# Two experts' weight units in runs of four in a two-layer encoder trunk

## The reference

```
logits = (t @ router)
top_v, top_i = lax.top_k(logits, TOP_K);  w = softmax(top_v)
for e in range(N_EXPERTS):
    out = out + combine[:, e:e + 1] * swiglu(t, w_gate[e], w_up[e], w_down[e])
swiglu(h, g, u, d) = (silu(h @ g) * (h @ u)) @ d        # g, u: 1024 x 3584, d: 3584 x 1024
```

## Time and profile before

| | us |
|---|---|
| median of 3 runs | 1401.47 |
| lowest, highest | 1400.12, 1403.07 |
| the profiled execution, device time | 1400.06 |
| its span, first to last instruction | 1398.0 |
| PE busy | 1369.0 (98%) |
| DVE busy | 737.5 (53%) |
| ACT busy | 632.1 (45%) |
| mean granted PE clock | 0.998 |

### The profile page before, as it was taken

The page is one execution under the profiler, slowest core; times in us unless marked ns, Lnnn a source line. Parts: engine busy times, 40 slices in busy tenths (PEclk is TensorE's granted clock), DMA queues, the critical chain, the costliest instruction groups (busy, mean ns, idle before and its releaser), DMA issues.

```text
span 1398.0 us, 16533 instructions
## 1 busy us (share of the span) xinstructions
PE 1369.0 (98%) x6427; PEld 928.7 (66%) x6427; DVE 737.5 (53%) x626; ACT 632.1 (45%) x574; POOL 28.9 (2%) x34
## 2 busy tenths in 40 slices
PE   7999999999999989999999999999999999999998
PEld 7978888888888865555565555565555556555555
DVE  6975544446733464554555554545545455455455
ACT  5855333444555345444444444444344445444443
POOL 2000000001200000000000000000000000000000
PEclk9999999999999999999999999999999999999999
DMA  9456555555440069999999999999999999999995
GB/s 335 166 178 229 180 181 186 196 190 163 149 141 1 15 253 409 412 415 415 399 414 398 365 413 413 407 399 393 362 404 413 406 410 397 374 387 414 414 399 245
DMA packets 127885, 434.83 MB, mean 311 GB/s; under 512 B 6960, under 2 KB 9120, under 8 KB 113472
## 3 DMA queue, kind: packets, MB, share of 16 engines
q1 hardware_dynamic: 127344, 433.11, 80.9%
q0 software_dynamic: 368, 0.63, 0.2%
q10 hardware_dynamic: 96, 0.03, 0.0%
HBM read 432.69 MB, written 1.05 MB: 310 GB/s over the span
## 4 chain that ended last, share of the span: by engine, by line
PE 82%; DMA 8%; ACT 4%; DVE 3%; issue 2%; DVEq 0%; SPq 0%; POOL 0%; ACTq 0%
PE ps L1320 18%; PE ps L1307 11%; PE ps L1308 9%; PE ps L838 9%; PE ps L1309 9%; PE ps L840 8%; PE ps L839 8%; DMA ring<-in_moe_w_gate_dram 5%; DVE wlo L1466 2%; DMA ring<-in_moe_w_down_dram 2%; ACT whi L487 2%; PE ps L1239 1%; PE ps L1230 1%; PE ps L1068 1%; DMA ring<-in_moe_w_up_dram 1%
## 5 line engine op out<-in xcount | busy, mean ns | idle before, releaser
L1466 DVE TENSOR_TENSOR wlo<-ring,whi 128x2048 fp32r<-128x2048 f32 x168 | 384.7, 2291 | 345.2 <-ACT whi L487 341.6
L487 ACT ACTIVATE whi<-ring 128x2048 fp32r<-128x2048 f32 x168 | 321.4, 1914 | 405.6 <-DMA ring<-in_moe_w_up_dram 153.4
L1320 PE MATMUL ps<-ring,xl 128*64 128x512 f32 (+1 forms) x1024 | 217.1, 550 | 2.3 <-issue 1.7
L1458 DVE TENSOR_TENSOR wlo<-raw,whi 128x2048 fp32r<-128x2048 f32 x73 | 166.5, 2288 | 73.5 <-PE ps L840 71.4
L1307 PE MATMUL ps<-whi,hT_hi 128*128 128x512 f32 x448 | 188.5, 421 | 8.4 <-DVE wlo L1466 7.7
L480 ACT ACTIVATE whi<-raw 128x2048 fp32r<-128x2048 f32 x73 | 139.4, 1916 | 84.8 <-PE ps L840 82.9
L1308 PE MATMUL ps<-wlo,hT_hi 128*128 128x512 f32 x448 | 177.1, 395 | 0.0
L1309 PE MATMUL ps<-whi,hT_lo 128*128 128x512 f32 x448 | 174.9, 390 | 0.0
L838 PE MATMUL ps<-whi,hT_hi 128*128 128x512 f32 x384 | 153.2, 399 | 2.4 <-DVE wlo L1458 1.4
L1307 PEld LDWEIGHTS ps<-whi,hT_hi 128*128 128x128 f32 x448 | 83.9, 187 | 105.8 <-issue 50.2
L840 PE MATMUL ps<-whi,hT_lo 128*128 128x512 f32 x384 | 149.7, 390 | 0.0
(11 more groups left out here) (312 smaller groups left out, 1328.0 us busy)
## 6 DMA issues: line engine op xcount, KB each, us to landing
ring<-in_moe_w_gate_dram SPq DMA_DIRECT2D x112, 1024.0 KB, 10.0
ring<-in_moe_w_up_dram SPq DMA_DIRECT2D x112, 1024.0 KB, 10.0
ring<-in_moe_w_down_dram SPq DMA_DIRECT2D x112, 1024.0 KB, 10.4
raw<-in_fox_w_in_dram SPq DMA_DIRECT2D x16, 1024.0 KB, 5.2
raw<-in_ffn_w_gate_dram SPq DMA_DIRECT2D x14, 1024.0 KB, 5.2
raw<-in_ffn_w_up_dram SPq DMA_DIRECT2D x14, 1024.0 KB, 5.1
raw<-in_ffn_w_down_dram SPq DMA_DIRECT2D x14, 1024.0 KB, 5.0
raw<-in_lru_w_in_dram SPq DMA_DIRECT2D x8, 1024.0 KB, 11.4
```

The lines of the kernel that those rows point to most:

```text
L487: nc.scalar.activation(whi[:, 1 + q % SPLIT], ring[:, i % RING], ACT.Copy).then_inc(hi_done, 1)
L1320: ins = mm(ps[g * HD:(g + 1) * HD, bank, 0:half], src(k), ring[:, i % RING, cols], start=first and k == 0, stop=last and k == tiles - 1, s ...
L1458: nc.vector.tensor_tensor(wlo[:, m % LR], raw[:, m % RR], whi[:, m % HR].bitcast(F32), ALU.subtract).then_inc(lo_done, 1)
L1466: nc.vector.tensor_tensor(wlo[:, q % SPLIT], ring[:, i % RING], whi[:, 1 + q % SPLIT].bitcast(F32), ALU.subtract).then_inc(lo_done, 1)
```

## The change

In `pair_table` the units of a stage come in runs of up to four: four of the small expert, then four of the large one. A stage of two steps (half down-projections, gate and up of the last chunk) has runs of two. As loads are issued, products made and roundings done in table order, all three change together. `i % 2` and `i // 2` are replaced by a list `HEAVY` of the large units' places. PE's stages go through the same generator `turns`, with each wait put at the first unit of its kind. Transposes of the small activations now follow the last small down unit, those of the large activations the large unit behind it. Some look-aheads are changed; `lo_to(unit("G", 1, 1, 0) + 2)`, DVE's `ahead` and the number of buffers are not.

```
-RING, SPLIT = 7, 3
+RING, SPLIT, RUN = 7, 3, 4
+def turns(steps):
+    for b in range(0, len(steps), RUN):
+        for job in (1, 0):
+            for n in steps[b:b + RUN]:
+                yield job, n
...
-        for n in steps:
-            for job in (1, 0):
-                place[kind, job, p, n] = len(units)
-                units.append((job, "GUD".index(kind), row + n * tiles, col, width))
+        for job, n in turns(steps):
+            place[kind, job, p, n] = len(units)
+            units.append((job, "GUD".index(kind), row + n * tiles, col, width))
...
+HEAVY = [i for i, unit in enumerate(TABLE) if unit[0] == 0]
+def freed(q):
+    return HEAVY[q - SPLIT] + 1 - (PAIR_UNITS if q < SPLIT else 0)
+LIGHT_DONE = PLACE["D", 1, PAIRS - 1, PAIR_U[PAIRS - 1] - 1] + 1
...                                                      # SP
-                        if before % 2:
-                            sp.wait_ge(lo_done, group.split(before // 2))
+                        if before % PAIR_UNITS in HEAVY:
+                            sp.wait_ge(lo_done, group.split(HEAVY.index(before % PAIR_UNITS)
+                                                            - (FFN_UNITS if before < 0 else 0)))
...                                                      # ACT, DVE the same
-                while 2 * nxt[0] + 1 <= min(n, PAIR_UNITS - 1):
-                    q, i = nxt[0], 2 * nxt[0] + 1
+                while nxt[0] < FFN_UNITS and HEAVY[nxt[0]] <= n:
+                    q, i = nxt[0], HEAVY[nxt[0]]
...
-                hi_to(1, following)
+                hi_to(HEAVY[0], following)
...
-                        hi_to(unit("G", 1, 1, 0) + 3, group)
+                        hi_to(unit("G", 0, 1, 0) + 2, group)
                         act_T_hi(group, 0)
...
+                        hi_to(unit("D", 1, p - 1, 3) + ahead, group)
+                        light_T_copy(group, p)
                         hi_to(unit("D", 0, p - 1, 2) + ahead, group)
-                        light_T_copy(group, p)
-                        hi_to(unit("D", 1, p - 1, 3) + ahead, group)
                         act_T_hi(group, p)
...                                                      # PE, gate of chunk p
-                    for n in range(PAIR_U[p]):
-                        if p and n == 0:
+                    for job, n in turns(range(PAIR_U[p])):
+                        if p and n == 0 and job == 1:
                             pe.wait_ge(l_silu, group.nth(p, PAIRS))
-                        half_unit(group, "G", 1, p, n)
...
+                        if p == 1 and n == 0 and job == 0:
                             pe.wait_ge(m_ST, group.nth(1))
                             act_transposes(group, 0)
+                        half_unit(group, "G", job, p, n)
...                                                      # PE, second half of the down-projection
-                        down_unit(group, 1, p - 1, 2)
-                        down_unit(group, 0, p - 1, 2)
-                        light_transposes(group, p)
-                        down_unit(group, 1, p - 1, 3)
-                        act_transposes(group, p)
-                        down_unit(group, 0, p - 1, 3)
+                        for job, n in turns(range(2, 4)):
+                            down_unit(group, job, p - 1, n)
+                            if n == 3 and job == 1:
+                                light_transposes(group, p)
+                            if n == 2 and job == 0:
+                                act_transposes(group, p)
...                                                      # PE, last down-projection
-                down_unit(group, 1, PAIRS - 1, 0)
-                down_unit(group, 0, PAIRS - 1, 0)
-                if following is not None:
-                    pe.wait_ge(m_xh, following.nth(1))
-                    gather(following, 1)
-                down_unit(group, 1, PAIRS - 1, 1)
+                for job, n in turns(range(2)):
+                    ...
+                        down_unit(group, job, PAIRS - 1, n)
+                    if following is not None and job == 0 and n == 0:
+                        pe.wait_ge(m_xh, following.nth(1))
+                        gather(following, 1)
...                                                      # DVE
-                lo_to(1, following)
+                lo_to(HEAVY[0], following)
                 light_rows(following)
...
-                            lo_to(unit("U", 0, 0, 2) + 2, group)
+                            lo_to(unit("U", 0, 0, 1) + 3, group)
                             one_hot(group)
```

More of the change, by code:

```diff
@@ L103, in pair_table @@
     assert len(units) == PAIR_UNITS == len(place)
-    assert all(unit[0] == 1 - i % 2 for i, unit in enumerate(units))
     return units, place
 TABLE, PLACE = pair_table()
+HEAVY = [i for i, unit in enumerate(TABLE) if unit[0] == 0]
 def at(count, per, i):
@@ L482, in hi_to @@
                     return
-                while 2 * nxt[0] + 1 <= min(n, PAIR_UNITS - 1):
-                    q, i = nxt[0], 2 * nxt[0] + 1
+                while nxt[0] < FFN_UNITS and HEAVY[nxt[0]] <= n:
+                    q, i = nxt[0], HEAVY[nxt[0]]
                     act.wait_ge(arrived[i % RING], group.landed(i))
-                    act.wait_ge(used, N_MOE if group is OPENING and q < SPLIT else group.units(i - 2 * SPLIT + 1))
+                    act.wait_ge(used, N_MOE if group is OPENING and q < SPLIT else group.units(freed(q)))
                     nc.scalar.activation(whi[:, 1 + q % SPLIT], ring[:, i % RING], ACT.Copy).then_inc(hi_done, 1)
@@ L780, in pair @@
                 if group is not OPENING:
-                    y_to_hi(1, group.units(-1), group.nth(0))
+                    y_to_hi(1, group.units(LIGHT_DONE - PAIR_UNITS), group.nth(0))
                     hi_to(5, group)
@@ L813, in _ @@
             nxt[0] = 0
-            hi_to(1, OPENING)
+            hi_to(HEAVY[0], OPENING)
             pair(OPENING, Group(0, 1))
@@ L821, in _ @@
             pair(last, None)
-            y_to_hi(1, last.units(PAIR_UNITS - 1), last.nth(1))
+            y_to_hi(1, last.units(LIGHT_DONE), last.nth(1))
             for h in range(2):
@@ L1280, in heavy_slots @@
             def heavy_slots(i):
-                return 1 + i // 2 % SPLIT, i // 2 % SPLIT
+                return 1 + HEAVY.index(i) % SPLIT, HEAVY.index(i) % SPLIT
             def last_unit(group, p, n):
@@ L1287, in last_unit @@
                 hs, ls = heavy_slots(i)
-                pe.wait_ge(lo_done, group.split(i // 2))
+                pe.wait_ge(lo_done, group.split(HEAVY.index(i)))
                 for h in range(2):
@@ L1345, in pair @@
                 for p in range(PAIRS):
-                    for n in range(PAIR_U[p]):
-                        if p and n == 0:
+                    for job, n in turns(range(PAIR_U[p])):
+                        if p and n == 0 and job == 1:
                             pe.wait_ge(l_silu, group.nth(p, PAIRS))
-                        half_unit(group, "G", 1, p, n)
-                        if p and n == 0:
+                        if p and n == 0 and job == 0:
                             pe.wait_ge(*((m_act, group.nth(1, PAIRS)) if p == 1 else (m_tlo, group.nth(p, PAIRS))))
-                        if p == 1 and n == 0:
+                        if p == 1 and n == 0 and job == 0:
                             pe.wait_ge(m_ST, group.nth(1))
                             act_transposes(group, 0)
-                        half_unit(group, "G", 0, p, n)
-                        if p == 1 and n == 0:
+                        half_unit(group, "G", job, p, n)
+                        if p == 1 and n == 0 and job == 0:
                             if group is not OPENING:
@@ L1365, in pair @@
                     else:
[L1366 to L1373, removed]
+                        for job, n in turns(range(0, 2)):
+                            if n == 0:
+                                pe.wait_ge((m_tlo, l_copied)[job], group.nth(p, PAIRS))
+                            down_unit(group, job, p - 1, n)
+                    for job, n in turns(range(PAIR_U[p])):
+                        if p and n == 0 and job == 1:
                             pe.wait_ge(l_act, group.nth(p, PAIRS))
-                        half_unit(group, "U", 1, p, n)
-                        if n == 0:
+                        if n == 0 and job == 0:
                             pe.wait_ge(m_silu, group.nth(p + 1, PAIRS))
-                        half_unit(group, "U", 0, p, n)
-                        if p == 0 and n == 1:
+                        half_unit(group, "U", job, p, n)
+                        if p == 0 and n == 1 and job == 0:
                             pe.wait_ge(*((m_col, 1) if group is OPENING else (m_acc, group.twice(1))))
@@ L1395, in pair @@
                     gather(following, 0)
-                down_unit(group, 1, PAIRS - 1, 0)
-                down_unit(group, 0, PAIRS - 1, 0)
```

(20 more changed lines are left out.)

## The result

The changed kernel takes 1455.2 us (median of 4; 1453.1 to 1457.9), the kernel before 1402.0 on the same chip: ratio 1.038, 95% interval 1.036 to 1.040. I had said 1428 and a range up to 1442. The sign was right; the forecast rise of 26 us was half of the measured 53.

The account below looks back on a forecast made before the run. Transfers bound long stretches, PE the starts of expert pairs. First group 2.3, three hand-overs at 7.7, 3 x (209.0 - 209.4) and tail 3.4 sum to 27.6 us on 1400.06: 1427.7, said as 1428, range 1404 to 1442.

Parts of the forecast that it names:

- All three stops: PE stalls in chunk 1, before the last down-projection and at the hand-over, from short look-aheads: 4.6, 3.9 and 4.1 us.
- The saving: Fewer small/large alternations on PE, 0.34 us each: 9.2 us less PE work per group, 37 over four groups.
- the walk: Step-by-step timing of one group: last load lands at P + 209.0, next group's first product 19.3 us later.
- S1: Chunk 1: DVE's look-ahead misses large unit 20, split only after act_T_lo; a PE stall of 4.6 us.
- the first group's 2.3: Cost of S1 in the first group, which starts transfer-bound: 2.3 us taken, inside bounds 0 and 5.75.
- P: PE's first product of a group, the zero point from which the walk counts its times.
- S3: Hand-over to the next expert pair: large-unit rounding and split, now waiting for load 4, precede xg_lo and light_rows; 4.1 us.
- The hand-over: From a group's last landing to the next group's first product: 19.3 us, before 11.6, costing 7.7 at each of three.
- The latency rule: Skill's 2.0 us plus bytes / 436e3, 4.4 for 1 MB, set aside for the trace's 5.7 to 7.7; 6.2 taken.
- (a): Rival: stalls cost nothing, switching saved removes the transfers' pauses in three groups; 1381, with half of it 1390; chance 0.12.
- (c): Rival: runs of four free ring slots in bursts, two more 2.5 us pauses per group's middle chunks; 1448; chance 0.08.

Follow-up runs that it names:

- e5_filled: Changed kernel, no look-ahead mended, throw-away PE products put under the waits at the three stops: 1437.2 us, ratio 1.025.
- e1_split20: Changed kernel with one line different: in chunk 1 DVE splits units 20 to 22 before act_T_lo: 1432.0 us, ratio 1.023.
- e3_rows_first: Changed kernel with gathered_lo ahead of the following pair's first large rounding and light_rows ahead of its split: 1437.6 us, ratio 1.026.

## Why the prediction was wrong

**The direction and the mechanism were right.** All three stops are where the forecast put them, released by the instructions it named, and taking the three away turns the loss into a gain. A fourth, before the first group's first large unit, it did not have.

**The saving was right.** With the stops gone PE's busy time is 36.5 us lower; the forecast had 37. A run of four small units takes 1035.66 - 1028.64 = 7.02 us; the walk had 7.0, with nothing lost at small-to-small edges. The Trainium skill, "TensorEngine Tiling (Array Packing)", section "Tiling Modes", says that a change of tiling mode, not just of tile, drains TensorE. The steps agree: 0.34 us per alternation before, and no step inside a run. The two forms also differ in type (fp32, fp32r), and no run parts the two.

**The failed step** is the price of a stop. The walk gave each stop its length and put the half clock behind it at nothing: "S1 gives unit 20 at 55.95. Four large ones and the small transposes (4 x 2.80 + 0.2 + 0.56) end at 67.9". A second step, the first group's 2.3, is below. Two stretches of the third group show the half clock. From P = 983.43 to the first unit of chunk 1 it was 1028.64 - 983.43 = 45.2 us, not 43.2: half clock behind S3. From unit 20 to the use of unit 24, which is the issue of load 31, it was 1057.2 - 1041.5 = 15.7, not 13.9: half clock behind S1. Load 31 and the group's last load, SyncE's issues with their landings:

```profile
L418 SPq DMA_DIRECT2D ring<-in_moe_w_up_dram x1: 372/372/372, 1057.2 to 1057.2; - x1
DMA to landing us min/median/max: 5.2/5.2/5.2
...
L418 SPq DMA_DIRECT2D ring<-in_moe_w_down_dram x1: 333/333/333, 1187.2 to 1187.2; - x1
DMA to landing us min/median/max: 10.5/10.5/10.5
```

Load 31 is issued at P + 73.8 (forecast 69.8), and the last load lands at P + 214.3 (forecast 209.0): 4.0 later by the issue, 1.0 earlier by the latency of 5.2 instead of 6.2, and 2.3 later because the 52 loads behind it took 135.3 instead of 133.0. The hand-over takes 21.8 (1197.7 to the next group's first product below) instead of 19.3; the forecast for S3 was 1.3 too short.

```profile
1219.51 2.83 PE L1334 MATMUL ps<-ring,xl 128*64 128x512 f32 x6 [5.34 <-DVE xl L1951]
```

**The sum by its terms.** By groups, from first product to first product, the last one to the end of the span (us); "filled" is `e5_filled`:

| group | before | changed | more | forecast | filled |
|---|---|---|---|---|---|
| first | 218.3 | 237.0 | 18.7 | 10.0 | 235.3 |
| second | 222.6 | 236.1 | 13.6 | 7.3 | 233.5 |
| third | 221.0 | 236.1 | 15.1 | 7.3 | 229.3 |
| last, with tail | 224.2 | 235.0 | 10.8 | 3.0 | 228.1 |

The first group's first product came 1.7 us earlier than before, which leaves the 56.5 us of the span. The first groups of the two kernels, before and after:

```profile
512.02 1.51 PE L1320 MATMUL ps<-ring,xl 128*64 128x512 f32 x6 [0.60 <-DVE xl L1943]
730.29 1.08 PE L1320 MATMUL ps<-ring,xl 128*64 128x512 f32 x4
...
510.28 1.08 PE L1334 MATMUL ps<-ring,xl 128*64 128x512 f32 x4 [0.61 <-DVE xl L1951]
747.29 1.12 PE L1334 MATMUL ps<-ring,xl 128*64 128x512 f32 x2 [4.60 <-DVE xl L1951]
```

Of the 29 us missing in all, the filled kernel gives 18 back: that part is the clock. Most of the remaining 11 is the first group, which is 17.1 us longer than before even when filled. There I took 2.3 for S1 inside bounds of 0 to 5.75, as something that the transfers would partly hide. PE stood 6.86 us, and taking this away (`e1_split20`) shortens this group by 7.0, from 237.0 to 230.0. The stop is longer than the others because ACT's three roundings, up to unit 22, stand ahead of its copy of the transposes, and here they wait for their landings: the transposes start at 562.02 and the copy only at 565.58, 3.6 us later instead of 1.3 in the third group (1035.66, 1036.93).

```profile
562.02 1.23 PE L1284 MATMUL ps<-ident,gt 128*128 128x128 f32 x8
563.77 1.91 ACT L501 ACTIVATE whi<-ring 128x2048 fp32r<-128x2048 f32 x1 [0.64 <-DMA ring<-in_moe_w_gate_dram]
565.58 1.00 ACT L763 ACTIVATE aT_hi<-ps 128x1024 fp32r<-128x1024 f32 x1
570.10 0.80 PE L1321 MATMUL ps<-whi,hT_hi 128*128 128x512 f32 x1 [6.86 <-DVE wlo L1474]
```

The short S3 and the slower 52 loads make up more of the 11; how much is theirs was not separated.

**The latency rule.** A load issued into an idle queue took 5.1 to 5.2 us (loads 7 and 31), below all of my 5.7 to 7.7, so this term erred the other way and hid a part of the rest. The estimate of 4.4, for GpSimd-issued transfers, from the Trainium skill ("DMA: Bandwidth & Descriptors", "Anatomy of one DMA") is still short of it, by 0.8; the measurement decides.

**The rivals.** (a), the free stalls: the gain from the switching saved shows once the stops are gone, at 1388.8 and not 1381; that the stops themselves are free was wrong. (c), bursts, gave a number (1448) close to the measured one by luck: with the stops mended, runs of four are the fastest of the lengths tried, and no loss to the bursts shows.

**The range** was too narrow because every end I varied was a duration of the kernel before. None was the state of an engine that the change makes stand for longer than it ever had: PE's longest stop in the middle of the expert part was 1.65 us, and it kept its clock: the mean granted clock of the execution was 0.998. That says what the clock is while PE is kept busy, not what it will be.

## What to carry to other kernels

When the order of work changes, look-aheads written as "so many units on" change their meaning; list every one, and check that the first unit needed is still within it and ahead of the next blocking task. A stop of an engine at the bound is to be priced at its length plus, where the granted clock falls, the half-speed stretch behind it: here S1's 4.6 us of stop cost PE some 6.5 (1.9 more over the units behind it), and throw-away products under the wait took part of the second back without shortening the wait. Grouping work by form is worth trying where two forms alternate and the trace shows a step between them, but its gain came only when nothing stood in its way: 37 us less PE work was 13 us of time. That the rest is held by the transfers is argued from their pace, not shown.

## What the runs showed of the hardware that I had not expected

A PE idle for 4.6 us came back at 1.2 GHz; idle for 0.45, or 1.65 at the loop's back edge before, it kept 2.4. In the mended kernel the back edge's 3.14 us was enough: the clock over the next 4 us was 0.57.

```profile
949.00:953.00 4.00, 4.00 (x12) 1.21 (x13) 2.27 (x2) 3.91 (x3) 0.00 (x0) 0.57 0.59 233
```

Around 2.4 us both happened, before the same unit of the second group. After 2.44 us in the changed kernel the clock stayed at 1.00; after 2.42 us in `e3_rows_first` it was 0.59. The length of the stop alone does not settle it, and what does is open here.

```profile
896.39 0.50 PE L1321 MATMUL ps<-whi,hT_hi 128*128 128x512 f32 x1 [2.44 <-DVE wlo L1474]
896.00:900.00 4.00, 3.61 (x16) 2.98 (x17) 3.64 (x4) 2.72 (x3) 0.00 (x0) 1.00 1.05 425
...
890.02 0.79 PE L1321 MATMUL ps<-whi,hT_hi 128*128 128x512 f32 x1 [2.42 <-DVE wlo L1474]
890.00:894.00 4.00, 3.98 (x11) 3.17 (x12) 3.68 (x3) 2.12 (x2) 0.00 (x0) 0.59 1.06 430
```
